# Expert weights of a mixture-of-experts stage, loaded as whole 16 KB rows instead of two 8 KB halves

## The reference, cut to what matters

```python
def expert_block(args):
    xb, e = args
    hid = jax.nn.silu(xb @ w_gate[e]) * (xb @ w_up[e])
    return hid @ w_down[e]
```

## Time and profile before

| | us |
|---|---|
| median of 3 executions | 1548.16 |
| lowest, highest | 1547.51, 1551.59 |
| the profiled execution, by the same clock as the median | 1550.22 |
| its span in the profile | 1548.4 |
| TensorE busy | 1470.8 (95%) |
| VectorE, ScalarE, GpSimd busy | 553.0, 456.8, 34.6 |
| queue of SyncE's DMAs, busy time as a share of 16 engines' span | 78.9% |
| DMA packets, bytes | 107058, 489.81 MB |
| matmuls of the gate and up products (L1552), of the down product (L1587) | 354.8 and 112.6, 226.8 |
| mean granted clock of TensorE | 0.985 |

### The profile page before, as it was taken

The page is one execution under the profiler, slowest core; times in us unless marked ns, Lnnn a source line. Parts: engine busy times, 40 slices in busy tenths (PEclk is TensorE's granted clock), DMA queues, the critical chain, the costliest instruction groups (busy, mean ns, idle before and its releaser), DMA issues.

```text
span 1548.4 us, 21198 instructions
## 1 busy us (share of the span) xinstructions
PE 1470.8 (95%) x8215; PEld 917.7 (59%) x8215; DVE 553.0 (36%) x858; ACT 456.8 (30%) x777; POOL 34.6 (2%) x41
## 2 busy tenths in 40 slices
PE   7999999999999999999999988988988989999997
PEld 5998989988889988643443332432432433444342
DVE  5755866553676868511111110110111111111112
ACT  5534655543555686311111110110111111111112
POOL 1000000000030000200000000000000000000000
PEclk9999999999999999999999999999999999999999
DMA  9564346554544324999999999999999999999996
GB/s 318 177 218 163 123 159 206 186 185 169 189 147 154 119 73 149 405 418 418 415 423 421 423 422 422 422 421 422 422 422 422 422 422 421 422 422 414 422 421 251
DMA packets 107058, 489.81 MB, mean 316 GB/s; under 512 B 9399, under 2 KB 11571, under 8 KB 60148
## 3 DMA queue, kind: packets, MB, share of 16 engines
q1 hardware_dynamic: 105460, 484.16, 78.9%
q0 software_dynamic: 1184, 4.26, 0.9%
q10 hardware_dynamic: 352, 0.54, 0.1%
HBM read 506.73 MB, written 1.08 MB: 328 GB/s over the span
## 4 chain that ended last, share of the span: by engine, by line
PE 74%; DMA 20%; DVE 2%; ACT 1%; issue 1%; SPq 1%; ACTq 0%; DVEq 0%
PE bank L1038 33%; PE bank L1552 21%; DMA slots<-in_w_up_dram 20%; PE bank L1587 9%; PE bank L1496 3%; PE bank L1506 2%; SPq L456 1%; PE bank L1028 1%; DVE xeT L2253 0%; PE bank L1379 0%; DVE w_split L1693 0%; PE bank L1123 0%; DVE h_lo L1683 0%; PE bank L1305 0%; PE bank L1114 0%
## 5 line engine op out<-in xcount | busy, mean ns | idle before, releaser
L1552 PE MATMUL bank<-slots,xeT 128*64 128x512 f32 x1536 | 354.8, 616 | 39.8 <-DMA slots<-in_w_up_dram 39.7
L1038 PE MATMUL bank<-h_hi,w_split 128*128 128x256 f32 x1504 | 278.7, 285 | 0.0
L1552 PEld LDWEIGHTS bank<-slots,xeT 128*64 128x64 f32 x1536 | 112.3, 142 | 276.9 <-issue 215.0
L1038 PEld LDWEIGHTS bank<-h_hi,w_split 128*128 128x128 f32 x1504 | 237.4, 193 | 2.5 <-issue 1.0
L1587 PE MATMUL bank<-slots,heT 128*64 128x512 f32 x1024 | 226.8, 595 | 8.0 <-ACT heT L959 8.0
L1693 DVE TENSOR_TENSOR w_split<-raw,w_split 128x2048 fp32r<-128x2048 f32 (+2 forms) x96 | 205.3, 2166 | 74.3 <-ACT w_split L624 74.1
L1038 PE MATMUL bank<-h_lo,w_split 128*128 128x256 f32 x752 | 213.3, 284 | 0.0
L624 ACT ACTIVATE w_split<-raw 128x2048 fp32r<-128x2048 f32 (+2 forms) x96 | 170.9, 1815 | 56.1 <-PE bank L1038 54.4
L2262 DVE TENSOR_TENSOR h_e<-bank,h_e 128x512 f32<-128x512 f32 x32 | 22.1, 692 | 421.4 <-PE bank L1552 421.4
L1587 PEld LDWEIGHTS bank<-slots,heT 128*64 128x64 f32 x1024 | 70.6, 137 | 145.3 <-issue 130.5
L1038 PEld LDWEIGHTS bank<-h_lo,w_split 128*128 128x128 f32 x752 | 144.9, 193 | 0.1
(11 more groups left out here) (353 smaller groups left out, 1374.9 us busy)
## 6 DMA issues: line engine op xcount, KB each, us to landing
slots<-in_w_up_dram SPq DMA_DIRECT2D x128, 1024.0 KB
slots<-in_w_down_dram SPq DMA_DIRECT2D x128, 1024.0 KB
areas<-in_w_gate_dram SPq DMA_DIRECT2D x64, 1024.0 KB, 17.9
slots<-in_w_gate_dram SPq DMA_DIRECT2D x64, 1024.0 KB
raw<-in_w_in_dram SPq DMA_DIRECT2D x42, 1024.0 KB, 5.7
raw<-in_w_ff_dram SPq DMA_DIRECT2D x32, 1024.0 KB, 5.3
raw<-in_w_out_dram SPq DMA_DIRECT2D x12, 1024.0 KB, 5.1
raw<-in_w_ple_gate_dram SPq DMA_DIRECT2D x4, 1024.0 KB, 5.6
```

What stands on the lines that cost most here:

```text
L1038: last = mm(psum, a[i][a_at], b[j][b_at], start=(start and n == 0), stop=(stop and n == 2), skip_group_check=shared)
L1552: last = mm(bank[SLOTS * e:SLOTS * e + SLOTS, :], xeT[:, k, odd, SLOTS * e:SLOTS * e + SLOTS], expert_panel(w, e, odd)[:, k, :], start=(k ...
```

## The change

Each expert's gate, up or down weights come in one DMA of 2 MiB whose rows are 16 KB, so that a panel of a pair is two DMAs instead of four. SyncE waits for the second of the two releases before the first of them; TensorE waits once, ahead of the product. Four loads keep the halves: gate 2 and down 1 (the first that wait for a release, written out ahead of the loop, which now starts at its second turn), and up 31 and down 31 (the last pair). TensorE's waits in the middle of a product remain only where such a load is: gate of even pairs from 2 on (against a constant that is reached by gate 2's second half), up of the last pair, down of odd pairs (the same). The order of the loads, the matmuls, the places and the bytes are as before. The later passes, for experts with more than 64 tokens, are changed alike and don't run on this input.

```diff
-            def load(w, i, pair, odd, beyond):
+            def load(w, i, pair, odd, beyond, in_halves=False):
...
-                rows = 2 if w == "down" else 4
-                for half in range(2):
+                rows = (4 if w == "down" else 8) // (2 if in_halves else 1)
+                for half in range(2 if in_halves else 1):
                     if not isinstance(i, int) or (w == "gate" and i > 1) or (w != "gate" and i > 0):
-                        sp.wait_ge(used, 2 * i - (3 if w == "gate" else 1) + half)
+                        sp.wait_ge(used, 2 * i - (3 if w == "gate" else 1) + (half if in_halves else 1))
...
-                def next_load(w, i):
-                    load(w, first + i, i, i % 2, beyond)
-
-                with sp.Fori(0, EARLY // 2) as j:
+                def next_load(w, i, in_halves=False):
+                    load(w, first + i, i, i % 2, beyond, in_halves)
+
+                opening = isinstance(first, int)
+                if opening:
+                    next_load("gate", 2, True)
+                    next_load("up", 1)
+                    next_load("down", 1, True)
+                    next_load("gate", 3)
+                    next_load("up", 2)
+                    next_load("down", 2)
+                with sp.Fori(1 if opening else 0, EARLY // 2) as j:
...
-                for w in ("gate", "up", "down"):
-                    next_load(w, PAIRS - 1)
+                next_load("gate", PAIRS - 1)
+                next_load("up", PAIRS - 1, True)
+                next_load("down", PAIRS - 1, True)
...
-                        if k % 4 == 0 and w == "gate":
-                            pe.wait_ge(pair_landed["odd_gate" if odd else w, k // 4], 32 * (couple + 1))
-                        elif k % 4 == 0:
-                            pe.wait_ge(pair_landed[w, k // 4], 32 * (i + 1))
+                        if k == 0 and w == "gate":
+                            pe.wait_ge(pair_landed["odd_gate" if odd else w, 0], 32 * (couple + 1))
+                        elif k == 4 and w == "gate" and not odd and not first_one:
+                            pe.wait_ge(pair_landed[w, 1], 32)
+                        elif k == 0 and w == "up":
+                            pe.wait_ge(pair_landed[w, 0], 32 * (i + 1))
+                        elif k == 4 and w == "up" and odd and last_one:
+                            pe.wait_ge(pair_landed[w, 1], 2 * (couple + 1))
...
-                pe.wait_ge(pair_landed["down", 1], 32 * (i + 1))
+                if odd and last_one:
+                    pe.wait_ge(pair_landed["down", 1], 2 * (couple + 1) + 32)
+                elif odd and isinstance(couple, int):
+                    pe.wait_ge(pair_landed["down", 1], 32)
```

More of the change, by code:

```diff
@@ L285, in program @@
         pair_landed = {(w, half): sem(f"{w}_{half}_landed") for w in ("gate", "odd_gate", "up", "down")
-                       for half in range(2)}
+                       for half in range(1 if w == "odd_gate" else 2)}
         picked, gathered, xe_a, xe_d = sem("picked"), sem("gathered"), sem("xe_by_scalar"), sem("xe_by_vector")
```

## The result

The changed kernel takes 1557.33 us in the median of 11 executions (1552.75 to 1559.07), the kernel before 1548.25 in 11 (1546.53 to 1551.59). The ratio is 1.0047, with a 95% interval of 1.0038 to 1.0056: **slower by 0.47%**, some 7 us. (The ratio is taken over all executions; the two medians alone lie 9.1 us apart.) The profiled execution took 1558.84 us, with a span of 1557.0 and a mean granted clock of 0.981; that is 8.6 us of span more than the one of before.

The account below looks back on a forecast made before the run. Expert-stage transfers were taken as the bound: byte rate and, in turn, whether late releases empty the queue. Terms +3.4 - 4.8 + 4.9 + 1.6 + 2.1 + 1.1 = +8.3 us, against median 1548.16, gave 1556.5; range 1547 to 1565.

Parts of the forecast that it names:

- Step 1, the rate: Expert-stage transfers: half as many packets, each 16 KB, save 0.95% (0.5% to 1.6%); 4.8 us back by pair 21's up product.
- the slope of 0.6 us for 0.1%: Each 0.1% of transfer rate moves the end by 0.6 us, over the stretches where rate and not release rules.
- the line through the 2 KB and 8 KB packets: Fixed time per packet, from full-engine windows: 3.1 ns with the best 2 KB microsecond, 9.1 ns with an 8 us mean.
- Step 2, the releases: Expert-stage refills wait for the whole old panel, 3.43 us later; the queue runs dry, pair 4's down panel starts 3.4 us later.
- the five places named: Places where the DMA share should fall below 1: near 704, 736, 757, then at 1403 and 1427 us.
- Step 3, the whole wait: Pair 21's up product waits for its whole panel, starts at 1260.9 and ends 3.5 us later, 1.7 us for lower clock.
- a second spell of low clock: Rival: behind each longer pause (some 5.5 us instead of 4.04) more low clock, +1.7 at pair 21's up product; 1558, chance 0.07.
- The tail: Last 290 us: later releases leave gaps; new waits at up 25 (2.2 us), down 28 (2.1) and gate 31 (1.1).
- the walk: Queue followed along SyncE's issue times through the expert stage, giving each gap and wait; end 8.3 us late.
- The sum: All terms over the whole kernel: +3.4 - 4.8 + 4.9 + 1.6 + 2.1 + 1.1 = +8.3 us.
- The 16 KB row is no cheaper: Rival: 16 KB rows are cut in the queue or their packets take twice as long; +16 us, 1564, chance 0.12.
- Faster: Rival: the queue never runs dry, only the 4.9 us whole wait is lost; from 1.5% rate on, 1543, chance 0.10.

Follow-up runs that it names:

- Experiment 1: Kernel before, loads in halves with 8 KB rows, but SyncE waits for the second release ahead of all four DMAs of a panel: 1556.33 us, ratio 1.0051.
- experiment 8: Changed kernel with the opening of before: halves up to pair 5, whole loads from pair 6 on (up 31, down 31 in halves): 1554.30 us, ratio 1.0035 to before.
- experiment 3: Changed kernel with 8 KB rows: same releases and waits, but each panel in four DMAs as before: 1565.79 us, ratio 1.0113 to the kernel before.
- experiments 4: Kernel before with whole 16 KB row loads for pairs 6 to 19 alone, halves elsewhere, SyncE and TensorE loops cut in three: 1545.67 us, ratio 0.9973.
- 9: Kernel before with whole loads for pairs 6 to 19, TensorE's loop left whole because SyncE raises the second count itself: 1545.15 us, ratio 0.9970.
- 10: Same as 9, plus whole loads for gate 20 to 27, up 20 and down 20: 1542.81 us, ratio 0.9958 to the kernel before.
- 5: Kernel before, but every expert's weights are loaded, also those without tokens (18 MiB more): 1590.29 us, ratio 1.0265 to before.
- 6: Changed kernel, but every expert's weights are loaded, also those without tokens: 1583.79 us, ratio 1.0223 to the kernel before.

## Why the prediction was right, point by point

Forecast 1556.5 and slower; measured 1557.33. The reasoning held in its parts, and two terms were mis-sized in opposite directions.

**Step 1, the rate: too small.** Forecast 0.95% (bounds 0.5 to 1.6%), measured 1.5%. By the slope of 0.6 us for 0.1% that is 3.3 us more given back. What was wrong is the weight given to the line through the 2 KB and 8 KB packets: taken back from the measured pair, 2 x 310.7 - 612 = 9.4 ns go with each packet that is saved and its share of the completion packets, which is close to the upper of the two estimates (9.1 ns), not to the lower (3.1). The mean over a loaded stretch was the nearer one, not the undisturbed microsecond. The fixed cost from the Trainium skill ("DMA: Bandwidth & Descriptors", section "Why small descriptors are slow") gave an estimate of 0.58%; the trace has two and a half times that, and the measurement decides.

**Step 2, the releases: right.** D4 issues at 755.32, 3.3 us late (forecast 3.4). The share falls at the five places named: 0.86, 0.66 and 0.68 in the windows above with 704, 1403 and 1427, and 0.94 and 0.95 in ten microseconds around 736 and 757. The opening's gaps, with the whole wait, also make TensorE wait one couple sooner, at U5 (1.93 us, at 787.82) instead of U7 (2.05 us, at 839.81). Experiment 1 adds what the sum did not price by itself: late releases alone are worth 8 us when no rate makes up for them.

The splitting rule of the Trainium skill ("Perfetto Trace Analysis", section "DMA Optimizations") names idle DMA engines as its condition, and by it no gap would have formed. The gaps formed: share 0.66 to 0.86 in the four windows. The engines were full right up to the place where smaller pieces were wanted.

**Step 3, the whole wait: right, the clock too small.** U21 starts at 1257.66, 0.3 us later than before, since the better rate brings the whole panel about when the first half came. It ends 1.6 us late instead of 3.5: 3.2 us less from the rate, 1.3 more from a product of 10.05 us where 8.78 was taken. The granted clock of 1240 to 1275 us is 0.90 in the mean (before: 0.95), so a larger part of it ran at 1.2 instead of 2.4 GHz. This is the rival "a second spell of low clock", which had come to 1.7. What the prediction left out of its picture of the pauses is that before, too, TensorE waits for the second halves of even pairs' up products (1.31 us at 874.60, for one). These small waits are gone, so in all TensorE's products from `slots` at this line wait 43.9 us where they waited 39.8, a tenth more; this changes no term of the sum.

**The tail: right in place, near in size.** Forecast ends or starts against measured: U25 +5.1 and +3.6, D28's start +7.2 and +5.2, G31's start +8.3 and **+8.6**. The first two are 1.5 and 2.0 us less than forecast, as U21's end was 1.9 less. Then the down product of pair 28 takes 8.76 us instead of 7.09 (granted clock 0.91 from 1450 to 1470 us): 1.7 us of low clock that the walk did not have, behind a wait of 2.00 us. In experiment 8 the same wait (2.01) is followed by a product at full clock, 7.09. What decides between the two is open. It may be part of why the executions of this kernel spread from 1552.75 to 1559.07: the four slowest have a mean granted clock of 0.981, the five fastest 0.983 to 0.985. But only one of them has a trace.

**The sum.** 8.3 - 3.3 (rate) + 1.3 (clock at U21) + 1.7 (clock at D28) = 8.0, measured 8.6 in the span. So the hit to 1 us is partly luck: a rate that was 0.55 points better and 3 us of clock cancelled.

**The rivals.** "The 16 KB row is no cheaper" had been put at 1564; the kernel that is just that, experiment 3, takes 1565.8. This agrees in the medians; its span is 14.4 us longer, under the 16 of that rival. "Faster" needed the queue never to run dry; experiments 4, 9 and 10 come near to that by choosing where to load whole (10 has one gap left, a share of 0.85 from 1405 to 1415 us), and 5 and 6 by taking the leads away, and each time the sign turns.

## What to carry to other kernels

A larger transfer needs a later release, and with one place per panel that release is worth nothing while the queue is deep, and where it is shallow its delay is lost nearly in full (a release 3.43 us later made D4 3.3 us late). Find from the trace where the consumer has a lead (here behind experts that are skipped) and keep small pieces there; use large rows where the consumer waits for the transfers, and let the last panel that it waits for come in pieces. A mixed version of this kernel was 0.4% faster than before, where the same change everywhere was 0.5% slower.

## What the runs showed of the hardware

- A 16 KB packet takes 612 ns of an engine where two of 8 KB take 621: 1.5% more bytes per microsecond (428 against 422 GB/s).
- Cutting loops is not free: the same work with two loops cut in three and eight more packets of instructions took 2.0 us longer (1.0013, 1.0004 to 1.0022). 1.3 us of it stand at one pause, behind the first new packets; later packets added almost nothing.
- Behind a pause of 4 us or more a product that takes 7.09 us at full clock takes 8.4 to 10.1 us in all the traces. Behind 2.0 us both 7.09 and 8.76 were seen, and behind 3.4 us 7.09 once (U7 of experiment 10) and 9.8 once (U7 of experiment 8).
